# Subtracting one weight piece on GpSimd in one instruction of 1024 columns instead of two of 512, in a two-layer hybrid trunk

## What is computed

```
u = layer_norm(x) * (1 + scale) + shift
parts = u @ w_in                      # q, k, v, gates and merge gates of three branches
qa = rope(rms_norm(qa) * gain)        # branch A; branch C has rope without the norm
ya = attention(qa, ka, va); ym = mlstm(...); yw = windowed_attention(...)
merged = sum(sigmoid(g_i) * ((y_i * silu(z_i)) @ w_branch[i]))
x = layer_norm(alpha * x + gate * (merged @ w_out)) * ln_g + ln_b
```

## Time and profile before

| | |
|---|---|
| median of three runs | 1801.54 us |
| the profiled execution's own time | 1804.96 us |
| its span in the trace | 1803.1 us |
| ACT busy | 475.1 us |
| DMA engines, mean over the span | 73 GB/s |
| mean granted TensorE clock | 0.961 |
| share of PE in the chain that ended last | 80% |

### The profile page before, as it was taken

The page is one execution under the profiler, slowest core; times in us unless marked ns, Lnnn a source line. Parts: engine busy times, 40 slices in busy tenths (PEclk is TensorE's granted clock), DMA queues, the critical chain, the costliest instruction groups (busy, mean ns, idle before and its releaser), DMA issues.

```text
span 1803.1 us, 21491 instructions
## 1 busy us (share of the span) xinstructions
PE 1625.7 (90%) x8235; PEld 1248.7 (69%) x8235; DVE 755.2 (42%) x1456; ACT 475.1 (26%) x1111; POOL 648.0 (36%) x511
## 2 busy tenths in 40 slices
PE   4898899999899999999548979999998999999994
PEld 0487678884588886787405867788746888877874
DVE  2348740355612334314623477403555124342155
ACT  0223740134600133301102237401355001332011
POOL 0255005530055443254602540145210554433555
PEclk8899999999999999999878999999999999999997
DMA  8421002212112222142054210022131222211411
GB/s 262 129 84 59 1 12 70 82 47 80 42 59 83 59 74 61 36 152 71 35 176 121 80 52 1 12 82 70 47 85 36 71 75 66 71 53 36 163 59 59
DMA packets 75880, 131.39 MB, mean 73 GB/s; under 512 B 16044, under 2 KB 20544, under 8 KB 75716
## 3 DMA queue, kind: packets, MB, share of 16 engines
q1 hardware_dynamic: 74728, 124.15, 22.5%
q10 hardware_dynamic: 1040, 5.77, 0.8%
HBM read 123.61 MB, written 8.92 MB: 73 GB/s over the span
## 4 chain that ended last, share of the span: by engine, by line
PE 80%; DVE 7%; ACT 3%; issue 3%; DMA 2%; SPq 2%; POOL 2%; POOLq 0%; ACTq 0%; DVEq 0%
PE pb L719 58%; PE pb L898 4%; PE pb L744 4%; PE pb L697 3%; PE pb L855 2%; DMA raw<-in_w_mod 2%; PE pb L817 2%; PE pb L824 1%; PE pb L828 1%; PE pb L935 1%; DVE rtmp L1554 1%; SPq L567 1%; POOL rstd L642 1%; DVE tokq L1539 1%; POOL xh L672 1%
## 5 line engine op out<-in xcount | busy, mean ns | idle before, releaser
L719 PE MATMUL pb<-wsp,act_T 128*128 128x512 f32 x4080 | 949.8, 393 | 10.9 <-issue 10.9
L719 PEld LDWEIGHTS pb<-wsp,act_T 128*128 128x128 f32 x4080 | 769.3, 189 | 176.8 <-issue 17.5
L654 POOL CAST wsp<-raw 128x1024 fp32r<-128x1024 f32 x152 | 163.5, 1076 | 1062.8 <-PE pb L719 858.2
L657 POOL TENSOR_TENSOR wsp<-raw,wsp 128x512 fp32r<-128x512 f32 x320 | 426.1, 1352 | 29.6 <-ACT wsp L1168 17.4
L719 PE MATMUL pb<-wsp,yT 128*128 128x512 f32 x720 | 169.9, 396 | 0.0
L697 PE MATMUL pb<-raw,csil 128*2 128x512 f32 x192 | 102.5, 653 | 61.9 <-DMA raw<-in_w_mod 59.5
L719 PEld LDWEIGHTS pb<-wsp,yT 128*128 128x128 f32 x720 | 135.5, 188 | 32.3
L1915 DVE SCALAR_TENSOR_TENSOR mt<-tg,pb 128x512 f32<-128x512 f32 x40 | 27.4, 684 | 268.2 <-PE pb L719 267.4
L1388 ACT ACTIVATE tg<-pb 128x512 f32<-128x512 f32 x60 | 35.9, 599 | 363.8 <-PE pb L719 363.8
L697 PEld LDWEIGHTS pb<-raw,csil 128*2 128x2 f32 x192 | 12.1, 86 | 124.8 <-DMA raw<-in_w_mod 85.9
L1236 ACT ACTIVATE pr<-pb,nm 128x640 f32<-128x640 f32 (+2 forms) x128 | 91.1, 712 | 2.0 <-DVE nm L1606 2.0
(11 more groups left out here) (242 smaller groups left out, 1636.3 us busy)
## 6 DMA issues: line engine op xcount, KB each, us to landing
raw<-in_w_in SPq DMA_DIRECT2D x112, 512.0 KB, 3.6
raw<-in_w_mod SPq DMA_DIRECT2D x48, 512.0 KB, 4.2
raw<-in_w_branch SPq DMA_DIRECT2D x24, 512.0 KB, 3.5
raw<-in_w_out SPq DMA_DIRECT2D x16, 512.0 KB, 3.5
out<-xh SPq DMA_DIRECT2D x10, 512.0 KB
raw<-in_w_in SPq DMA_DIRECT2D x16, 256.0 KB, 3.3
xh<-out SPq DMA_DIRECT2D x2, 2048.0 KB, 8.7
xh<-in_x_sample ACTq DMA_DIRECT2D x1, 2048.0 KB, 8.5
```

The costliest lines, as they stand in the source:

```text
L654: pool.tensor_copy(hi, raw[:, p % 3, :, 0:width]).then_inc(pool_step, 1)
L657: ins = pool.tensor_tensor(lo[:, j, :], raw[:, p % 3, j, 0:width], hi[:, j, :].bitcast(F32), ALU.subtract)
L719: mm = pe.matmul(dst, lhs(a, k, t), wsp[:, piece % 2, w, j, 0:width], start=(k == 0 and n == 0), stop=(i == count - 1 and j == 1 and n == 2))
```

## The change

The loop over the two blocks of a piece is gone. One instruction subtracts the whole piece, 128 partitions by 2 by 512, and raises `raw_used`. What is computed is the same.

```
--- before.py
+++ after.py
@@ -653,9 +653,8 @@
                         copies += 1
                         pool.tensor_copy(hi, raw[:, p % 3, :, 0:width]).then_inc(pool_step, 1)
                         pool.wait_ge(pool_step, copies)
-                    for j in range(2):
-                        ins = pool.tensor_tensor(lo[:, j, :], raw[:, p % 3, j, 0:width], hi[:, j, :].bitcast(F32), ALU.subtract)
-                    ins.then_inc(raw_used, 1)
+                    pool.tensor_tensor(lo, raw[:, p % 3, :, 0:width], hi.bitcast(F32), ALU.subtract)\
+                        .then_inc(raw_used, 1)
                     if p == pieces.first[("A", "q")] + 2:
                         inv_sqrt(rmsk[:, :], msk[:, :], 2)
                     if p == pieces.first[("A", "z")] + 1:
```

## The result

The kernel after the change takes 1812.54 us (median of 11 runs, 1806.18 to 1815.93), the one before 1801.59 us (11 runs, 1799.55 to 1804.96). The ratio of the two is 1.0056, with a 95% interval of 1.0044 to 1.0069. It is slower by 0.56%, which is outside both the forecast of 1801.2 us and its range. The profiled execution took 1812.43 us, with a span of 1810.6 us and a mean granted clock of 0.957 (0.961 before).

A forecast was written before the change was run, and what follows sets the result against it. PE was taken as the bound, with POOL trailing it. Per layer -0.32 + 0.35 - 0.16 = -0.13 us, twice -0.3 us, took 1801.54 to 1801.2 us, range 1797.5 to 1805.0 us.

The forecast's parts named there:

- What bounds the kernel: Whole kernel: PE never waits for a split; POOL trails it and idles 3.13 us per piece of the output product.
- The price of the instruction: Each subtraction on POOL: 2.34 us for 1024 columns, 0.16 to 0.21 us less per piece; POOL busy about 596 us.
- Layer start: First two splits of a layer: two pairs each 0.16 us shorter end VectorE's hold earlier, a gain of 0.32 us a layer.
- Branch A: Queries and z, six splits with VectorE on the path: PE's wait for L1568 ends 0.35 us later in each layer.
- walk by rows: Branch A, VectorE followed row by row through the holds: L1523 held 1.05 us longer, ending 0.35 us late a layer.
- `rms` slack: Branch A, VectorE's 0.60 us wait for `rms`: it swallows 0.6 to 0.7 us of lateness, leaving about 0.3 us.
- mLSTM: Start of the mLSTM, where L1836 is held by a pair: the pair ends 0.16 us earlier, a gain per layer.
- Elsewhere the splits meet no waited-for VectorE work: All other places, attention and a layer's tail included: no split delays VectorE work that is waited for, no term.
- Rival 1: Branch A: long holds cost 1.05 us per VectorE arrival, 1813 us; chance 0.09 for 1 to 5 us lost, 0.03 over 5.4.
- The SBUF page: The skill's rule of an exclusive lock for the whole instruction: longer instructions mean longer blocks for whoever comes second; no size.

The follow-up runs named there:

- run 5: The kernel before, with one instruction only for the pieces from a layer's start to the second of branch A's `G`: 1804.2 us against 1801.19, ratio 1.0016.
- Run 2: The kernel before, with only the first two output pieces of each layer subtracted in one instruction: 1810.55 us against 1802.25, ratio 1.0042.
- run 1: The changed kernel, with the first two output pieces of each layer subtracted in two halves again: 1805.55 us against 1802.25, ratio 1.0016.
- run 9: The kernel before, with one fill of `mt` on VectorE between the last tile merged and the copies of the transposed merge: 1803.89 us against 1801.31, ratio 1.0013.
- runs 3 and 11: The changed kernel, with the first output piece's subtraction waiting for the merge (1803.33 us), or with the first two `G` pieces of branch A split after `q_ready` (1801.76 us).

## Why the prediction was wrong, step by step

- **What bounds the kernel** was right. PE never waited for a split, and POOL's idle time per piece of the output product went from 3.13 to 3.29 us (forecast: over 3.2):
```profile
877.23 1.04 POOL L654 CAST wsp<-raw 128x1024 fp32r<-128x1024 f32 x1 [3.29 <-PE pb L718]
878.35 2.39 POOL L656 TENSOR_TENSOR wsp<-raw,wsp 128x1024 fp32r<-128x1024 f32 x1
```
- **The price of the instruction** was right: 2.36 to 2.40 us undisturbed against 2.34. The busy time, 611.7 us against 596, was missed because the disturbed ones raise the mean to 2.44.
- **Layer start**: forecast -0.32 us a layer. From the transposes of the modulation to the first product it was 13.08 and 13.18 us before and is 13.01 and 12.68 after, so -0.07 and -0.50. The sum of both, -0.57 against -0.64, is close.
- **Branch A**: forecast +0.35 us a layer, measured +0.19 at PE's wait:
```profile
128.08 2.59 DVE L1522 TENSOR_TENSOR rtmp<-tokq 128x512 f32<-128x512 f32 x1 [0.40 <-ACT tokq L1183]
...
134.46 1.71 DVE L1525 TENSOR_SCALAR ms<-ms 128x8 f32<-128x8 f32 x1
...
157.41 2.85 DVE L1553 TENSOR_TENSOR rtmp<-tokq,rope 128x256 f32<-128x256 f32 x2
...
169.05 1.94 PE L743 MATMUL pb<-ident,tokq 128*128 128x128 f32 x8 [6.76 <-DVE zt L1567]
```
  The walk by rows held: L1522 stands 2.59 us where L1523 stood 1.50, 1.09 longer and not the 1.05 of the walk, and the `rms` slack gave most of it back. But run 5 prices branch A and layer start together at 1.6 thousandths, 3 us (1.3 to 4.3). That is more than the 0.4 us of two waits, and this difference isn't settled.
- **mLSTM**: forecast -0.16 us, measured 1.75 to 1.62, -0.13.
- **"Elsewhere the splits meet no waited-for VectorE work"** is the step that failed. It was a term of zero, and it was asserted and not looked up. The first two output pieces are split just when branch B's last product ends, and VectorE's additions there are waited for. The term is 2.68 us in the first layer and 3.30 in the second, up to the first output product. Behind it the slower matmuls add 56.44 - 54.69 = 1.75 us in the first layer and nothing in the second. That makes 7.7 us of the 10.9 between the medians. Run 2 prices it at 5.2 to 10.1 us (0.0029 to 0.0056 of 1802), and run 1 shows the reverse.
- **The clock** had no term in the sum either. The second layer shows that the term at the merge tail isn't a fixed one: the same pause costs 4.43 us with what follows it in the first layer and 3.30 in the second.
- **Rival 1** had the right mechanism, a long hold that slack doesn't give back, in the wrong place. Its 1813 us agrees with the measured 1812.5 by chance: it came from 12 splits of branch A at 1.05 us each, and the loss comes mainly from four splits of the merge tail. The prediction gave 0.03 to a loss over 5.4 us. That was too little, as the trace has places that were not walked.
- **The SBUF page**: the Trainium skill (SBUF — State Buffer, section "Who interferes with whom") adds that the order of issue decides who blocks. The trace agrees, and this half of the rule was the one needed: 0.81 us for an addition that starts 0.34 us ahead of POOL, 2.14 us for one that starts 1.10 us behind it. I had used the rule on durations only, and not asked whose turn would change.

## What to carry to other kernels

A split on GpSimd, subtraction or cast, is for VectorE's work with two inputs from SBUF a door that stays shut for its whole length: the held additions end 0.54 us behind the POOL instruction, 821.94 behind 821.40 and 829.24 behind 828.69. VectorE's instructions that take one of their inputs from a bank of `pb` aren't held (0.67 to 0.69 us for L1914), nor is a fill (0.91 us, run 9). But the tiny L1525, with one input, was (1.71 us; undisturbed 0.17). Merging two into one saves 0.15 us on POOL and doubles the worst wait of the neighbour, so look wherever that neighbour works at PE's pace with PE waiting behind it, above all at the end of a product. List those places for every split before putting a zero on "elsewhere". And the cheaper way round isn't the length of the instruction but its time: where a split isn't urgent, let it wait until the neighbour is done (1787.2 us against 1801.2).

## What the runs showed of the hardware that I had not expected

- Two collisions do more together than apart: 0.9998 for the second alone, 1.0022 for the first alone, 1.0042 for both. The first shifts VectorE by 1.1 us, which is more than the 0.34 us by which the second was avoided, and on the way VectorE meets the cast between them as well.
- The clock's answer to a pause didn't follow from the pause alone: none at 1.86 and 2.07 us; behind 3.15 us 0.51, 0.54 and 0.60 over 7 us, but 0.76 in the second layer of the changed kernel; and 0.76 over 7 us around 4.25 us. Where the low stretch falls counts as much as its length. Where it reached into the output product it slowed the matmuls there, by 1.75 us in the changed kernel's first layer. In its second layer, and at 4.25 us, it lay in the pause and the transposes and slowed the output matmuls not at all. Why the same pause has two answers isn't shown.
- Not explained: in the one profile after, attention in layer 1 has a low-clock stretch of 3.4 us near 463 us that layer 2 and the profile before don't have. PE is 1.9 us later at its end than before, 0.3 us of that from ahead of it. The next low stretch, near 493 us, lasts 6.8 us instead of 3.4. No other profile has either, not even those of runs 3 and 11, in which every split is wide. So the wide form doesn't bring them by itself, and I take them for a variation from run to run, which wasn't tried.
